# RWKV's triangular inverse on compact 64x64 diagonal blocks, in matmuls of 32 stationary columns

## The reference

```python
def step(S, inp):
    r_t, w_t, k_t, v_t, kk_t, a_t = inp
    sa = -jnp.einsum('bhvk,bhk->bhv', S, kk_t)
    S = (S * w_t[:, :, None, :] + sa[..., None] * (kk_t * a_t)[:, :, None, :]
         + v_t[..., None] * k_t[:, :, None, :])
    return S, jnp.einsum('bhvk,bhk->bhv', S, r_t)
```

## Time and profile before

| | |
|---|---|
| median of 3 runs | 1389.52 us (1388.11 to 1390.04) |
| the profiled execution | 1388.51 us |
| its span | 1386.7 us |
| PE busy, DVE busy, ACT busy, POOL busy | 1279.2, 682.2, 421.6, 518.6 us |
| the mix of layer 1 with the inverses (636 to 965 us): PE, DVE busy | 272.18, 234.47 us |
| mean granted clock of PE | 0.967 |

### The profile page before, as it was taken

One profiled execution on the slowest core, in us unless ns is written; L12 is line 12 of the kernel. 1 busy time (PEld: TensorE's weight loads), 2 busy tenths in 40 slices (PEclk: granted clock), 3 DMA queues, 4 the chain that ended last, 5 costly groups with the idle time before them and its releaser, 6 DMA issues.

```text
span 1386.7 us, 21884 instructions
## 1 busy us (share of the span) xinstructions
PE 1279.2 (92%) x9060; PEld 1038.0 (75%) x9060; DVE 682.2 (49%) x992; ACT 421.6 (30%) x536; POOL 518.6 (37%) x374
## 2 busy tenths in 40 slices
PE   5999999999999999979798888787899999999997
PEld 4797978888888888856666656564688888888885
DVE  7435365551124444457758587675655511244334
ACT  4547333221122222253334324222432211222110
POOL 4341435554445555431121030110245544455541
PEclk9899999999999999989999999897999999999998
DMA  4331212222322223210011010000022232222221
GB/s 183 115 107 46 77 72 96 91 91 100 112 91 91 91 91 105 101 67 32 32 34 50 11 50 14 31 33 1 28 95 91 91 105 108 91 91 91 94 88 61
DMA packets 16808, 105.74 MB, mean 76 GB/s; under 512 B 1872, under 2 KB 2144, under 8 KB 4832
## 3 DMA queue, kind: packets, MB, share of 16 engines
q1 hardware_dynamic: 16304, 104.03, 21.1%
q10 hardware_dynamic: 432, 0.64, 0.1%
HBM read 102.57 MB, written 2.10 MB: 75 GB/s over the span
## 4 chain that ended last, share of the span: by engine, by line
issue 50%; PE 27%; POOL 21%; DVE 1%; DMA 0%; POOLq 0%; ACT 0%; SPq 0%; DVEq 0%
PE ps L861 23%; POOL w_lo L501 21%; PE ps L946 3%; PE ps L915 1%; DMA w_raw<-in_weights 0%; DVE x L1361 0%; PE ps L896 0%; POOL w_lo L490 0%; POOLq L495 0%; ACT w_hi L601 0%; POOLq L498 0%; SPq L454 0%; DVE xsq L1372 0%; DVE scaled L1431 0%; DVE x L1433 0%
## 5 line engine op out<-in xcount | busy, mean ns | idle before, releaser
L501 POOL TENSOR_TENSOR w_lo<-w_raw,w_hi 128x512 fp32r<-128x512 f32 x368 | 509.6, 1415 | 827.5 <-ACT w_hi L514 284.1
L861 PE MATMUL ps<-h_hi,w_hi 128*128 128x512 f32 x696 | 283.7, 408 | 11.6 <-POOL w_lo L490 11.6
L861 PE MATMUL ps<-h_lo,w_hi 128*128 128x512 f32 x696 | 275.0, 395 | 0.0
L861 PE MATMUL ps<-h_hi,w_lo 128*128 128x512 f32 x696 | 274.8, 395 | 0.0
L861 PEld LDWEIGHTS ps<-h_hi,w_hi 128*128 128x128 f32 x696 | 132.8, 191 | 51.3 <-issue 12.2
L589 ACT ACTIVATE w_hi<-w_raw 128x2048 fp32r<-128x2048 f32 x50 | 95.7, 1914 | 194.7 <-PE ps L861 143.4
L861 PEld LDWEIGHTS ps<-h_hi,w_lo 128*128 128x128 f32 x696 | 132.8, 191 | 28.7
L861 PEld LDWEIGHTS ps<-h_lo,w_hi 128*128 128x128 f32 x696 | 133.3, 192 | 25.9 <-issue 0.5
L861 PE MATMUL ps<-f_hi,w_lo 128*128 128x512 f32 x384 | 149.5, 389 | 0.0
L861 PE MATMUL ps<-f_hi,w_hi 128*128 128x512 f32 x384 | 149.5, 389 | 0.0
L861 PE MATMUL ps<-f_lo,w_hi 128*128 128x512 f32 x384 | 149.5, 389 | 0.0
(11 more groups left out here) (305 smaller groups left out, 1941.9 us busy)
## 6 DMA issues: line engine op xcount, KB each, us to landing
w_raw<-in_weights SPq DMA_DIRECT2D x93, 1024.0 KB, 4.9
outT<-x SPq DMA_DIRECT2D x8, 256.0 KB, 2.0
x<-in_xT SPq DMA_DIRECT2D x6, 256.0 KB, 7.3
masks_f<-in_masks SPq DMA_DIRECT2D x1, 768.0 KB, 10.6
x<-in_xT ACTq DMA_DIRECT2D x2, 256.0 KB, 5.6
w_raw<-in_weights SPq DMA_DIRECT2D x1, 512.0 KB, 6.4
low_w<-in_low_w SPq DMA_DIRECT2D x1, 512.0 KB, 11.3
sgu_ln<-in_sgu_ln SPq DMA_DIRECT2D x1, 512.0 KB, 3.6
```

Source lines behind the costliest of these rows:

```text
L501: piece = pool.tensor_tensor(w_lo[:, j, at], w_raw[:, j, at], w_hi[:, j, at].bitcast(f32), SUB)
L861: mm = pe.matmul(bank(gb(g) if isinstance(i, int) else g % 2), w, r, start=(k == 0 and m == 0), stop=(k == K - 1 and m == 2))
```

## The change

Until level 6 an inverse is two independent 64x64 blocks. They are now kept compact: xc, xtc and txc are 64 columns for each matrix, partitions 0 to 63 hold the upper block and 64 to 127 the lower one. Each block's product is cut in two output halves of 32: four matmuls for each matrix (QUARTERS), each with 64 rows, 32 stationary columns and 32 moving columns, on four tiles along the array's diagonal, where there were two of 128 rows. XT's part of dx is a step of its own, dxt, for all eight matrices, behind both halves of dx; the next tx waits for X alone (x_upd), the next dx for XT (xt_upd). Products are in other banks, alternating by level. DVE's copies are 128x128 for each half of X and 128x256 for all of XT. Level 6 joins the two blocks: one matmul of 64 rows, 64 stationary and 64 moving columns for each matrix in tx and in dx, and ACT makes the full 128x128 XT: two copies of the diagonal blocks, and one of the corner for each half; g waits for these (xt_last, xt_diag). XT's lower left corner is zeroed once. The order of the other steps stays, except that at (c, level) = (0, 2), (1, 2) and (2, 3) the planner now puts an evacuation (evac_a, evac_b) between dx and dxt. The masks of the levels are 32 source columns wide where they were 64, and level 6 has none: the mask DMA falls from 1536 to 1024 columns.

```diff
@@ -19,6 +19,7 @@
 EXP_HALF = float(np.exp(-0.5))
 LEVELS = 7
 COLUMN_HALVES = [slice(0, 64), slice(64, 128)]
+QUARTERS = [(h, slice(a, a + 32)) for h in COLUMN_HALVES for a in (h.start, h.start + 32)]
 
 
...
@@ -50,7 +51,7 @@
 
 MSRC, MCOLS = {}, {}
 for _name, _n, _times in [("gla", 128, 2), ("score", 256, 2), ("reset64", 128, 4), ("reset128", 128, 4)] \
-        + [(f"lvl{a}{lv}", 64, 4) for lv in range(LEVELS) for a in ("X", "XT")]:
+        + [(f"lvlX{lv}", 32, 4) for lv in range(LEVELS - 1)] + [(f"lvlXT{lv}", 32, 8) for lv in range(LEVELS - 1)]:
     MSRC[_name] = (sum(n for _, n in MSRC.values()), _n)
     MCOLS[_name] = (sum(n for _, n in MCOLS.values()), _n * _times)
...
@@ -175,9 +176,11 @@
             btok = sb("btok", [P, TT, P])
             ktok = sb("ktok", [P, TT, P])
             SC = sb("SC", [P, 8, 512])
-            X = sb("X", [P, 8, P])
             XT = sb("XT", [P, 8, P])
-            TX = sb("TX", [P, 8, P])
+            xc = sb("xc", [P, 8, 64])
+            xtc = sb("xtc", [P, 8, 64])
+            txc = sb("txc", [P, 8, 64])
+            ident64 = sb("ident64", [P, 64])
             low0 = sb("low0", [P, SEQ])
             low1 = sb("low1", [P, SEQ])
...
         block = ctx.enter_context(nc.Block())
 
-        def half_of(t, b, B, side):
-
-            v = t[:, :, :].rearrange("p y (q h b) -> p (y q) h b", h=2, b=B)
-            q = P // (2 * B)
-            return v[:, 4 * b * q:4 * (b + 1) * q, side, :]
-
-        def half_of_one(t, yy, B, side):
-            return t[:, yy, :].rearrange("p (q h b) -> p q h b", h=2, b=B)[:, :, side, :]
-
-
+        def sides(t, a, b, B, side):
+
+            v = t[:, a:b, :].rearrange("p y (q h b) -> p (y q) h b", h=2, b=B)
+            return v[:, :, side, :]
+
+        def side_of_one(t, r, yy, B, side):
+            return t[r, yy, :].rearrange("p (q h b) -> p q h b", h=2, b=B)[:, :, side, :]
+
+        def tx_bank(lv, b):
+
+            return (2, 3)[b] if lv % 2 else (4, 5)[b]
+
+        def x_bank(lv, b):
+
+            return (4, 5)[b] if lv % 2 else (2, 3)[b]
+
+        def xt_bank(lv):
+            return tx_bank(lv, 0)
 
...
             ORDER1 += taps[0]
             for lv in range(1, LEVELS):
                 ORDER1 += [("tx", c, lv, 0), ("tx", c, lv, 1)] + mid[lv] + fill(LEVEL_N[c][lv - 1])
-                ORDER1 += [("dx", c, lv, 0), ("dx", c, lv, 1)] + end[lv] + taps[lv]
+                ORDER1 += [("dx", c, lv, 0), ("dx", c, lv, 1)]
+                if lv < LEVELS - 1:
+                    ORDER1 += [("dxt", c, lv)]
+                ORDER1 += end[lv] + taps[lv]
             for n in range(TT):
                 ORDER1 += [("g", c, n)] + fill(STATE_N[c][2 * n]) + [("u", c, n)] + fill(STATE_N[c][2 * n + 1])
...
+                    act.wait_ge(s("ident64_done"), 1)
                     if c:
-                        act.wait_ge(s("y_mm"), 4 * c)
-                    for t in (X, XT):
-                        act.activation(t[:, :, :], mats[:, 0:1, :].broadcast_to([P, 8, P]), ACT.Copy).then_inc(s("x_id"), 1)
+                        act.wait_ge(s("xt_upd"), 5 * c)
+                        act.wait_ge(s("tx_mm"), 12 * c)
+                        act.wait_ge(s("dx_mm"), 12 * c)
+                        act.wait_ge(s("xt_diag"), 2 * c)
+                    for t in (xc, xtc):
+                        act.activation(t[:, :, :], ident64[:, :].rearrange("p (y n) -> p y n", y=1).broadcast_to([P, 8, 64]),
+                                       ACT.Copy).then_inc(s("x_id"), 1)
                 if i == 5:
                     for b, (dst, name) in enumerate(((vtok, "vtok_done"), (btok, "btok_done"), (ktok, "ktok1_done"))):
...
@@ -769,8 +788,27 @@
                 B = 1 << lv
                 at = (c * 6 + lv - 1) * 2 + b
                 act.wait_ge(s("tx_mm"), at + 1)
-                act.activation(half_of(TX, b, B, 0), as2(bank(2 + b, 0, 256), B), ACT.Copy)\
-                   .then_inc(s("tx_done"), 1)
+                if lv == LEVELS - 1:
+                    act.activation(txc[64:128, 4 * b:4 * b + 4, :],
+                                   ps[64:128, tx_bank(lv, b), 0:256].rearrange("p (y n) -> p y n", n=64), ACT.Copy)\
+                       .then_inc(s("tx_done"), 1)
+                else:
+                    act.activation(sides(txc, 4 * b, 4 * b + 4, B, 0), as2(bank(tx_bank(lv, b), 0, 128), B), ACT.Copy)\
+                       .then_inc(s("tx_done"), 1)
+
+            def dx(c, lv, b):
+                if lv < LEVELS - 1:
+                    return
+                if b == 0:
+                    act.wait_ge(s("xt_upd"), 5 * c + 5)
+                    if c:
+                        act.wait_ge(s("y_mm"), 4 * c)
+                    act.activation(XT[0:64, :, 0:64], xtc[0:64, :, :], ACT.Copy).then_inc(s("xt_diag"), 1)
+                    act.activation(XT[64:128, :, 64:128], xtc[64:128, :, :], ACT.Copy).then_inc(s("xt_diag"), 1)
+                act.wait_ge(s("dx_mm"), 12 * c + 10 + b + 1)
+                act.activation(XT[0:64, 4 * b:4 * b + 4, 64:128],
+                               ps[0:64, x_bank(lv, b), 0:256].rearrange("p (y n) -> p y n", n=64), ACT.Copy)\
+                   .then_inc(s("xt_last"), 1)
 
             def g_(c, n):
...
@@ -1175,8 +1213,8 @@
                 for n in range(TT) if i == 4 else ():
                     for h2, r in enumerate(COLUMN_HALVES):
                         for to in COLUMN_HALVES:
-                            mm = pe.matmul(ps[to, 3 + h2, 64 * n:64 * n + 64], AR[r, c % 2, n, 0, to],
-                                           bT[r, n * P:n * P + P:2], start=True, stop=True)
+                            mm = pe.matmul(ps[to, 3 + h2, 32 * n:32 * n + 32], AR[r, c % 2, n, 0, to],
+                                           bT[r, n * P + to.start:n * P + to.stop:2], start=True, stop=True)
                 if i == 4:
                     mm.then_inc(s("L_mm"), 1)
...
@@ -1195,35 +1233,57 @@
 
                 B = 1 << lv
                 if lv == 1:
-                    pe.wait_ge(s("x_init"), 2 * c + 2)
+                    pe.wait_ge(s("x_init"), 4 * c + 2)
                     pe.wait_ge(s("ktok1_done"), c + 1)
                 else:
-                    pe.wait_ge(s("xt_upd"), (6 * c + lv - 2) * 2 + b + 1)
+                    pe.wait_ge(s("x_upd"), (5 * c + lv - 2) * 2 + b + 1)
                 for yy in range(4 * b, 4 * b + 4):
-                    for r in COLUMN_HALVES:
-                        mm = pe.matmul(as2(ps[r, 2 + b, 64 * (yy % 4):64 * (yy % 4) + 64], B), SC[:, yy, r],
-                                       half_of_one(X, yy, B, 0), start=True, stop=True)
+                    at = yy % 4
+                    if lv == LEVELS - 1:
+                        mm = pe.matmul(ps[64:128, tx_bank(lv, b), 64 * at:64 * at + 64], SC[0:64, yy, 64:128], xc[0:64, yy, :],
+                                       start=True, stop=True)
+                    else:
+                        for r, to in QUARTERS:
+                            mm = pe.matmul(as2(ps[to, tx_bank(lv, b), 32 * at:32 * at + 32], B), SC[r, yy, to],
+                                           side_of_one(xc, r, yy, B, 0), start=True, stop=True)
                 mm.then_inc(s("tx_mm"), 1)
 
             def dx(c, lv, b):
 
                 B = 1 << lv
                 pe.wait_ge(s("tx_done"), (6 * c + lv - 1) * 2 + b + 1)
+                if lv == 1:
+                    pe.wait_ge(s("x_init"), 4 * c + 4)
+                else:
+                    pe.wait_ge(s("xt_upd"), 5 * c + lv - 1)
                 for yy in range(4 * b, 4 * b + 4):
-                    at = 64 * (yy % 4)
-                    if lv < LEVELS - 1:
-                        for r in COLUMN_HALVES:
-                            pe.matmul(as2(ps[r, 4 + b, at:at + 64], B), XT[:, yy, r], half_of_one(TX, yy, B, 0),
-                                      start=True, stop=True)
-                    for r in COLUMN_HALVES:
-                        mm = pe.matmul(as2(ps[r, 4 + b, 256 + at:320 + at], B), TX[:, yy, r], half_of_one(XT, yy, B, 1),
+                    at = yy % 4
+                    if lv == LEVELS - 1:
+                        mm = pe.matmul(ps[0:64, x_bank(lv, b), 64 * at:64 * at + 64], txc[64:128, yy, :], xtc[64:128, yy, :],
                                        start=True, stop=True)
+                    else:
+                        for r, to in QUARTERS:
+                            w = slice(to.start - r.start, to.stop - r.start)
+                            mm = pe.matmul(as2(ps[to, x_bank(lv, b), 32 * at:32 * at + 32], B), xtc[r, yy, w],
+                                           side_of_one(txc, r, yy, B, 0), start=True, stop=True)
                 mm.then_inc(s("dx_mm"), 1)
+
+            def dxt(c, lv):
+
+                B = 1 << lv
+                pe.wait_ge(s("tx_done"), (6 * c + lv - 1) * 2 + 2)
+                for yy in range(8):
+                    for r, to in QUARTERS:
```

(62 more changed lines are left out.)

## The result

| | before | after | predicted |
|---|---|---|---|
| median of 5 runs, us | 1389.52 | 1381.78 (1379.87 to 1384.41) | 1360.5 (1351 to 1377) |
| span of the profiled execution, us | 1386.7 | 1380.0 | about 1357.7 |
| tx 1 to g, c = 0 to 3, us | 43.04, 45.85, 39.86, 29.79 | 37.33, 40.31, 39.23, 34.36 | -8.7, -8, -8, -6.5 |

The ratio is 0.9942 [0.9926, 0.9958]: faster, by 7.7 us of the 29 forecast, and outside the range. The four stretches from the first product of level 1 to g sum to 158.5 us before and 151.2 after, 7.3 less; the span fell by 6.7. (The forecast's figures count in part from a little earlier, as the windows of the earlier trace rows do: from there these went from 174.6 to some 164 us, about 10 less.)

The account below looks back on a forecast made before the run. PE's small matmuls were taken to pace some inverse levels and DVE's queue others. Savings of 31.2 us over four stretches, less 2 us given back, were set at -29: 1360.5 us, range 1351 to 1377.

Parts of the forecast that it names:

- The pitch: Small matmuls of levels 1 to 5: a record every 8.5 ns on four diagonal tiles, 15.5 as the other end.
- The work of DVE: Copies of X halve, XT takes one copy, level 6 moves to ACT: DVE's queue shrinks by some 18 us.
- the rate of the small matmuls: PE, levels 1 to 5: 192 records a level at 8.5 ns cost 1.63 us, against 2.84 for 96 before.
- so issue keeps up at least at that rate beyond 32 records: PE's instruction supply: read from a burst of 128 records, 13.4 ns each at half clock.
- the sum: Savings over the four inverse stretches: -8.7 us in c=0, -8 each in c=1 and c=2, -6.5 in c=3; -31.2 together.
- What gives back: PE idles longer where DVE paces, more than half of each c=3 level, risking low clock: 2 us allowed.
- Rival 3: Matmuls get faster but each saved stretch becomes a wait for DVE, ACT or weights: 1388 us; chance 0.04.
- Rival 1: Issue or 64-row tiles hold the pitch at 13.4 to 15.5 ns: -14 to -19 us, about 1373; chance 0.2.
- signs of being wrong: Pitch above 10 ns, tx waiting for dxt's copy, or the four stretches shrinking by less than 25 us together.
- The planner's change: Evacuation before dxt at three places: xt_upd some 2.5 us later, but DVE paces there; its copy costs 0.35 us alone.

Follow-up runs that it names:

- halves: Changed kernel with 64 stationary columns, each block's product whole, in all of levels 1 to 5: 1388.11 us, ratio 0.9979.
- the fillers: Five unread full-array fp32 matmuls, one behind each dxt of c=3: 1372.34 us with whole products in c=3, 1379.07 on the changed kernel with quarters.
- c3halves: Changed kernel with each block's product whole (64 stationary columns) in c=3 alone, quarters in c=0 to 2: 1378.09 us, ratio 0.9893.
- rows128: As c3halves, but c=3 reads operands from all 128 rows, summing the two blocks: 1375.01 us, one run.
- mix: Against the kernel with whole products and five wide matmuls in c=3: dxt alone also whole in c=0 to 2: 1373.84 us, ratio 0.9876.
- plan: Against the kernel with whole products and five wide matmuls in c=3: planner's three evacuations put behind dxt again: 1374.04 us, ratio 0.9869.
- b_tiny: Kernel before the change with 24 tiny matmuls added ahead of each dx half in c=3: 1395.25 us, one run.

## Why the prediction was wrong

**The pitch was right.** 8.5 ns forecast; 8.8 to 9.3 measured for bursts of 61 to 64 records, 13.4 at half clock. Four diagonal tiles into one bank overlap, as argued from the earlier trace rows: one 64x64 tile at a time takes 61.5 ns for 64 moving columns, so half of them on two tiles at a time would give some 15 ns, an estimate, and 8.8 is well under it. So the rule of the Trainium skill (TensorEngine Tiling (Array Packing), Restrictions and Gotchas) doesn't hold for tiles on different output partitions in this trace either.

**The work of DVE was right.** Its busy time fell by 18.8 us over the program (682.2 to 663.4), forecast some 18. From dx 1 (649.84) to tx 4 (665.66, above) 15.8 us, forecast 16.0 to the copies and some 16.2 to tx 4; two X copies 0.48 us, for 0.4. The 16 records of level 6 come 61.5 ns apart (59 forecast); the wait before g is 0.47 us for ACT. c=0 gave 5.7 of 8.7.

**The step that failed** is the sentence in the part on the rate of the small matmuls, "so issue keeps up at least at that rate beyond 32 records". It took a burst of 128 records for a lasting rate. A burst can run to the end of the block of 256 instructions that has arrived; what lasts is 30 ns a record, weight load included. Priced so, 192 records of a level need 5.8 us of supply for 2.9 before, in place of the 1.63 of the sum, and a level of c=3 took 5.1 us before. The 2089 instructions of c=3 alone need 31.5 us at that rate, an estimate, where 29.79 were measured before and 23.3 forecast. The trace of before held the hint: its transfers stand 4.8 to 10 us apart in c=3, and nothing in the sum asked how close they can come. The Trainium skill (Runtime: NRT & Kernel Launch, Instruction fetch mechanics) says that instructions are streamed in blocks of 256 and that crossing a block's end is mostly hidden, because dispatch is slower than the fetch. The block size agrees with this trace (254 to 259 instructions between gaps); that it is hidden doesn't, with gaps of 0.34 to 2.09 us in c=3 and bursts at 4.5 ns an instruction for 15 of supply. By that rule the change would have kept its gain.

**The term that was mis-sized** is the clock in "What gives back", 2 us. The forecast saw that PE would idle more in c=3, and priced that alone. The granted clock of c=3 fell from 1.00 to 0.68: 1.2 GHz from 910.5 to 924.1 and again from 927.5 us; ahead of the first fall PE had been idle 1.42 us for issue and 1.38 for DVE within 4 us, and the fall is in the second of them. The price of the clock in halves is 6.4 us (34.08 to 27.71 with the fillers, no gaps in either). In quarters it isn't known: the fillers gave back 1 us net, with their own time in it. In halves the 64 rows of the tiles are a cause beside idle time: c3halves was busy 92% of the stretch at 0.64, rows128 80% at 0.89. For the quarters this was not tried.

**By stretch.** c=3 was forecast at -6.5 and came at +4.6: there 7.8 us of gaps and the low clock count, since no projection is left between the levels; without both, in halves and with fillers, it took 27.71, 6.7 less. c=2, -0.6 for -8, lost 5 us in the two places shown above, each one gap and a stretch at 0.50; the other 2.4 us were not traced. For c=0 and c=1, with 3.5 us of gaps each, the missing 2.5 to 3 us are near that sum, but some of these gaps are free, as seen above, and in mix what their removal gave was taken back by dxt in halves and the clock; how much of the 2.5 to 3 is gap and how much clock stays open. What quarters would give without the limit on the supply was not tried.

**What held besides.** Rival 3 had the sign of what happened (a saving turned into a wait) but named the wrong waits: nothing waits for DVE, ACT or weights that did not before. Rival 1 asked whether issue holds the pitch at 13.4 to 15.5 ns, in which case 1373; the limit acts on the stream at 30 ns a record, twice that. Of the signs of being wrong it was the last that came: the four stretches shrank by less than 25 us; the pitch stayed under 10 ns and tx waited for no copy of dxt. The planner's change was put at its copy alone; plan, 1374.04 for 1374.09, shows no more than that.

## What to carry to other kernels

Count instructions as well as time: before a matmul is cut in smaller ones, divide the length of the stage by the instructions in it, weight loads included, and look in the trace at how close the instruction transfers already stand. Use narrow tiles where other work on the engine stretches the stage (c=0: 37.3 us with quarters, 43.4 with halves), and wide ones where the small matmuls are all there is (c=3 with fillers: 27.7 with halves, 33.4 with quarters). And read the granted clock of each stage of the kernel after: a few useless full-array matmuls may be worth more than the edit (here five of them shortened c=3 by 6.4 us in halves, by 1 us in quarters).

## What the runs showed of the hardware

- TensorE's instructions arrive in blocks of 256, at the closest 3.3 to 4.2 us apart in these stretches, some 15 ns for an instruction; PE resumes 2.2 to 2.5 us behind the start of the transfer, and a gap of "issue" of 0.2 to 2.1 us is how it shows. With half the instructions there is none (halves). The same limit acts with 128-row tiles (b_tiny).
- Pitch of fp32 records at full clock: 8.8 to 9.3 ns with 32 stationary columns on four diagonal tiles, 28 to 31 with 64 on two, 61.5 with 64 on one; at 1.2 GHz 13.4 for the first and 52 for the second.
- The mean clock of c=3 was 0.64 in c3halves, with PE busy 31.4 of 34.1 us on tiles of 64 rows; the same columns over 128 rows had 0.89 (one run), and with five full-array matmuls beside the 64 rows it was 1.00.
